# A hybrid decoder step: a planner that also keeps VectorE's time, and S5 steps cut into smaller units

## What is computed

```python
hn = rmsnorm(x, ln1_g)
proj = hn @ w_in                                    # q | k | v | u, 512 columns each
a = p[:, :, 0] - lam * p[:, :, 1]                   # differential attention, 4 heads, causal
...
_, h = lax.associative_scan(combine, (a, bu), axis=1)   # S5, 32 groups, 64 complex states
...
x = x + jnp.concatenate([attn, s5_out], axis=-1) @ w_out
x = x + hier_moe(rmsnorm(x, ln2_g), ...)            # 1 of 4 groups, 2 of 8 experts in it
```

## Time and profile before

| | us |
|---|---|
| median of 3 runs | 1464.19 (1458.98 to 1472.08) |
| the profiled execution | 1464.86 |
| its span, first to last instruction | 1463.1 |
| TensorE / VectorE / ScalarE busy | 1279.2 / 521.6 / 248.5 |

### The profile page before, as it was taken

How to read it: one execution, slowest core, us unless ns; L and a number is a source line. 1 busy time by engine, 2 the same in 40 slices (tenths; PEclk the granted TensorE clock), 3 DMA queues, 4 the chain that set the end, 5 groups by cost and what they waited for, 6 DMA issues and landing times.

```text
span 1463.1 us, 26568 instructions
## 1 busy us (share of the span) xinstructions
PE 1279.2 (87%) x9000; PEld 670.6 (46%) x9000; DVE 521.6 (36%) x1413; ACT 248.5 (17%) x476; POOL 214.7 (15%) x329
## 2 busy tenths in 40 slices
PE   7999999999869799998869999976899999999930
PEld 4545555554324346666544444433444444444410
DVE  2723543253365455553512111153122111121126
ACT  2101111121212233332212000000011111111111
POOL 2003140313100200000010000001122222222211
PEclk9999999999989999998999999976999999999975
DMA  9989998869968999999996998998899999999764
GB/s 364 329 310 293 321 294 283 272 198 298 298 227 304 352 338 363 365 315 323 331 387 228 330 336 293 322 349 321 277 324 371 360 354 363 361 363 366 256 211 179
DMA packets 185201, 458.31 MB, mean 313 GB/s; under 512 B 23953, under 2 KB 24337, under 8 KB 176530
## 3 DMA queue, kind: packets, MB, share of 16 engines
q1 hardware_dynamic: 163602, 390.21, 75.4%
q0 software_dynamic: 21504, 66.78, 13.8%
HBM read 421.92 MB, written 33.80 MB: 311 GB/s over the span
## 4 chain that ended last, share of the span: by engine, by line
PE 70%; DMA 12%; DVE 7%; SPq 5%; issue 3%; DVEq 2%; ACT 1%; POOL 0%; ACTq 0%; POOLq 0%
PE WA L1800 52%; PE SC L1800 7%; PE OD L1800 7%; DMA ring<-in_cacheK 6%; SPq L500 4%; DMA qpad<-h_scratch,idc 3%; DMA ring<-in_cacheV 2%; PE WA L2166 2%; DVE arena L1769 1%; PE WA L1919 1%; DVE arena L1782 1%; DVE st L1141 1%; PE WA L2126 1%; DMA arena<-y_scratch 1%; DVEq L1771 1%
## 5 line engine op out<-in xcount | busy, mean ns | idle before, releaser
L1800 PE MATMUL WA<-arena 128*128 128x512 f32 (+10 forms) x1440 | 353.4, 432 | 17.6 <-issue 7.2
L1800 PE MATMUL WA<-arena,xm 128*128 128x512 f32 (+3 forms) x816 | 313.6, 581 | 8.4 <-DMA arena<-in_w_out 6.5
L1800 PEld LDWEIGHTS WA<-arena 128*128 128x128 f32 (+2 forms) x1440 | 191.6, 195 | 155.0 <-issue 135.5
L1800 PEld LDWEIGHTS WA<-arena,xm 128*128 128x128 f32 (+1 forms) x816 | 124.4, 174 | 162.8 <-issue 154.7
L1800 PE MATMUL WA<-xm,arena 128*128 128x512 f32 x192 | 87.3, 603 | 1.7 <-ACT arena L958 1.3
L1800 PE MATMUL OD<-ring,sall 128*32 128x512 f32 x512 | 71.0, 670 | 15.0 <-DMA ring<-in_cacheV 15.0
L563 POOL TENSOR_TENSOR st<-st,consts 128x1 f32<-128x1 f32 (+2 forms) x18 | 13.8, 765 | 466.2 <-DVEq L1175 280.0
L1800 PE MATMUL OD<-ring,qpad 128*32 128x128 f32 x2048 | 67.9, 285 | 15.7 <-DMA ring<-in_cacheK 15.7
L1800 PEld LDWEIGHTS OD<-ring,qpad 128*32 128x32 f32 x2048 | 56.6, 114 | 35.9 <-DMA ring<-in_cacheK 18.4
L1800 PE MATMUL SC<-ring,qpad 128*32 128x128 f32 x2048 | 64.9, 278 | 9.1 <-DMA ring<-in_cacheK 9.0
L1712 DVE TENSOR_TENSOR xm<-WA,colw 128x960 f32<-128x960 f32 x16 | 18.5, 1158 | 147.2 <-PE WA L2166 147.2
(11 more groups left out here) (364 smaller groups left out, 1244.1 us busy)
## 6 DMA issues: line engine op xcount, KB each, us to landing
ring<-in_cacheK SPq DMA_DIRECT2D x512, 256.0 KB, 4.7
ring<-in_cacheV SPq DMA_DIRECT2D x512, 256.0 KB, 4.7
arena<-in_w_gu SPq DMA_DIRECT2D x16, 2048.0 KB, 9.8
arena<-in_w_dn SPq DMA_DIRECT2D x16, 1024.0 KB, 14.3
ring<-in_w_gu SPq DMA_DIRECT2D x8, 2048.0 KB, 10.3
xm<-in_w_gu SPq DMA_DIRECT2D x8, 2048.0 KB, 10.5
ring<-in_w_dn SPq DMA_DIRECT2D x8, 1024.0 KB, 14.8
xm<-in_w_dn SPq DMA_DIRECT2D x8, 1024.0 KB, 14.8
```

The lines of the kernel that those rows point to most:

```text
L1800: return pe.matmul(out, lhsT, rhs, start=first, stop=last, **kw)
```

## The change

- The planner now keeps a second clock, `busy`, for VectorE. `vector_us` gives each unit's time on VectorE and a lag from TensorE's end to its start; the end is written down as `("dve",) + unit`, and other units can name it as what they wait for. So a unit on VectorE is late when those ahead of it on VectorE are late.
- The lags in `streams` are cut down to what lies between VectorE's end and the next step. Some TensorE costs change (`O` from 0.37 to 0.21 per block, `bY` 3.5 to 4.1, `ids` 5.5 to 6.9).
- `hold` counts from VectorE's end where the unit has one.
- `s5a` becomes four units, `bA` two and `bH` three (`p` is the part). The instructions and their semaphores stay the same; between two parts other units may stand.
- ScalarE's order puts `S` by VectorE's end.

```diff
+def vector_us(unit):
+
+    k, a = unit[0], unit[1:]
+    i = a[0] if a else 0
+    if k in ("u", "k", "q", "out") and (len(a) == 1 or a[-1] == 1):
+        return {"u": (1.1, 0.2), "k": (1.25, 0.95), "q": (1.25, 0.95), "out": (0.75, 0.2)}[k]
+    return {
...
+        "S": (1.95 + 0.265 * i, 0.2), "C": (0.95 + 0.133 * i, 0.0), "O": (1.35 if a[1:] == (H - 1,) else 1.15, 0.2),
...
+        "bH": ((3.7, 3.0, 5.6)[a[1] if k == "bH" else 0], 0.0), "bY": (0.75, 0.9), "bG": (0.75, 0.8),
...
-        C.append((("C", i, h), 0.0, [(("S", i, h), 3.3 + 3.0 * w)]))
...
-        O.append((("O", i, h), 0.2 + 0.37 * (i + 1), x))
...
+        C.append((("C", i, h), 0.0, [(dve("S", i, h), 0.9 + w)]))
...
+        O.append((("O", i, h), 0.2 + 0.21 * (i + 1), x))
...
-    return {"S": 3.0 + 3.0 * w, "T": 0.5 + 0.8 * w, "O": 0.5, "pt": 1.3, "bY": 5.0, "bP": 1.5, "bK": 1.6,
-            "bX": 0.8, "q": 0.8, "k": 0.8, "v": 0.8, "hT": 1.5, "out": 1.0}.get(k, 1.0)
+    k, w = unit[0], 0.115 * (unit[1] + 1) if len(unit) > 1 else 0
+    return {"S": 0.7 + w, "T": 0.5 + w, "O": -0.5, "pt": 1.3, "bP": 1.5, "bK": 1.0, "out": 0.1, "u": 0.1, "hT": 0.1, "r": 0.1,
+            "bX": 0.8, "q": -0.4, "k": -0.4, "v": 0.9, "ot": 1.4, "glu": -0.8, "ids": 4.0, "rank": 16.0}.get(k, 1.0)
...
         t = max(t, ready) + cost
-        end[unit] = t
+        end[unit] = done = t
+        if vector_us(unit):
+            us, lag = vector_us(unit)
+            end[("dve",) + unit] = done = busy = max(busy, t + lag) + us
...
-                free[b] = t + hold(unit)
+                free[b] = done + hold(unit)
...
-    ready = {u: ends.get(u, ends.get(u[:-1], 0.0)) + (2.4 if u[0] == "S" else 0.0) for u in PLAN}
+    ready = {u: ends[("dve",) + u] - (0.9 + 0.13 * u[1]) if u[0] == "S" else ends.get(u, ends.get(u[:-1], 0.0)) for u in PLAN}
...
-            def bH(n):
+            def bH(n, p):
...
+                if p == 1:
+                    for j in range(JQ):
+                        decay = r8[:, JQ * n + j:JQ * n + j + 1].to_broadcast([128, NC])
+                        dve.tensor_tensor_scan(A[:, j, :], decay, X[1][:, j, :], 0.0, MUL, ADD)
+                        dve.tensor_tensor_scan(B[:, j, :], decay, X[0][:, j, :], 0.0, MUL, ADD)
+                    dve.drain()
+                    return
```

More of the change, by code:

```diff
@@ L125, in streams @@
         qs += [(("q", i, 0), half, x), (("q", i, 1), half, [])]
-    qt = [(("qt", i), 0.6, [(("q", i, 1), 3.5)] + ([(("S", i - 1, H - 1), 0)] if i else [])) for i in range(NT)]
+    qt = [(("qt", i), 0.5, [(dve("q", i, 1), 0.3)] + ([(("S", i - 1, H - 1), 0)] if i else [])) for i in range(NT)]
     S, C, T, O = [], [], [], []
@@ L144, in streams @@
+    s5 = [(("s5a", 0), 0.0, [(dve("dprep"), 0.0)])] + [(("s5a", p), 0.0, [(dve("s5a", p - 1), 1.3)]) for p in range(1, 4)]
     for n in range(NQ):
[L145 to L148, removed]
@@ L187, in make_plan @@
     land, gone, due = [4.0, 10.0], [], 4.0
-    kept, never = {}, 1e9
+    kept, never, busy = {}, 1e9, 0.0
     def place(unit):
@@ L226, in make_plan @@
         for b in kept.get(unit, []):
-            free[b] = t + 1.0
+            free[b] = done + hold(unit)
         if unit[0] in "KV":
@@ L1264, in cmul, with s5a_parts @@
                 dve.drain()
-            def s5a():
+            def s5a_parts():
                 dve.wait_ge(s_ld5, 32)
@@ L1329, in s5a @@
                 dve.drain()
+                yield
                 a, b = (v[7], v[6]), (v[18], v[19])
@@ L1354, in s5a, with bA @@
                     a, b = b, a
[L1356 to L1362 removed]
+                    if tab is T1 and k == 4:
+                        yield
+                yield
+            s5a_part = s5a_parts()
+            def s5a(p):
+                next(s5a_part)
+            def bA(n, p):
                 j = slice(JQ * n, JQ * n + JQ)
                 full = [128, JQ, CH, W5]
[L1365 removed]
                 Lj = [Lp[:, m, :, j].rearrange("p k j -> p j k") for m in range(2)]
[L1367 to L1369 removed]
+                if p == 0:
+                    if n:
+                        dve.wait_ge(*filled("Y", n - 1, 1))
+                    else:
+                        dve.wait_ge(*filled("u", 3, 1))
+                        dve.wait_ge(s_ust[1], 32)
+                    t = [tmp5[:, 512 * m:512 * m + 512].rearrange("p (j r h) -> p j r h", j=JQ, r=CH) for m in range(2)]
+                    cmul([PB[:, m, :, :, :] for m in range(2)],
+                         [bc[:, 0, m, j, :].unsqueeze(2).to_broadcast(full) for m in range(2)],
+                         [x[:, :, 0:CH].unsqueeze(3).to_broadcast(full) for x in Lj], t)
+                    dve.drain().then_inc(s_pA, 1)
+                    return
                 for m in range(2):
```

124 lines of the change are left out of this document (64 added, 60 removed), and 3 rows, old and new, of the table i.

## The result

The changed kernel takes 1476.46 us (median of 9 runs, 1473.44 to 1479.97) against 1464.19 for before (median of 9 runs, 1458.98 to 1472.08). The ratio is 1.0098, 95% interval 1.0071 to 1.0125. Run again beside other kernels (experiment e12) it is 1.0068 (1.0035 to 1.0101). So the change makes the kernel slower, by 0.7 to 1 %. The forecast was 1443 us, with 1467 as its upper end.

A forecast was written before the change was run, and what follows sets the result against it. The prediction took TensorE, busy 87% of the span, and its stalls as the bound. Terms -14.3 - 2.1 - 4 - 0 - 1.5 = -21.9 from 1464.9 gave 1443.0 us; own range 1433 to 1453, with rivals 1425 to 1467.

The forecast's parts named there:

- The third stage: Second K pass with the big heads: transfers set its length, TensorE's gain waits for pages; 0, bounds 0 and -7.
- What bounds the kernel now: Planned part: TensorE, busy 87%, idle 104.5 us; largest single stall 11.1 us, a long S5 unit ahead of attention.
- The T stalls: Transposes of weighted probabilities: all three waits go because bH(3) and bE(3) move ahead of the heads; -14.3 us.
- The clock: Matmuls just behind the 11.1 us stall: their slow running goes with the stall; -2.1 us, bounds 0 and 4.
- Page units earlier: K units of both passes: work moved behind them fills gaps where pages are late; -4 us, bounds 0 and -10.5.
- The last stage: Second V pass: an output half moves ahead, a V unit behind r(7); -1.5 us, bounds -5.5 and +3.
- A: Rival: pages take it back, K units wait longer by the 10.5 us they moved forward; 1457.5 us, chance 0.20.
- B: Rival: VectorE's waits get into the S5 chain, six units at 8.1 us; slower, 1491.6 us, chance 0.10.
- C: Rival: stage three's transpose waits (7 us) and 10 us of page waits go as well; 1426 us, chance 0.12.
- D: Rival: nothing moves, the stall goes and the next page unit waits as much; 1464 us, chance 0.08.
- The closing test of the prediction: Planned part: T waits gone and first second-pass K unit early, but same end, means stages three and four were misjudged.

The follow-up runs named there:

- e12: The changed kernel, unchanged, run once more beside the others on the same chip; 1474.66 us, ratio 1.0068.
- e11: The order of before with the last round's three bH parts spread behind C(1,0), C(1,1) and AN(0); 1458.72 us, ratio 0.9962.
- e15: e11 with bH(3)'s second part directly behind its first, both behind C(1,0); 1459.91 us, ratio 0.9975.
- e6: The changed kernel with `ids` one V unit later, so two V units stand behind it; 1470.84 us, ratio 1.0053.
- e14: The changed kernel with the edits of e13 and e6 together; 1459.59 us, ratio 0.9983.
- e13: The changed kernel with two V units of the first V pass (and ov(1)) one projection half later; 1470.57 us, ratio 1.0060.
- e10: The changed planner with VectorE's clock, but the parts of s5a, bA and bH placed directly behind one another; 1492.03 us, ratio 1.0170.
- e3: The order of before up to the first V unit of the second pass, the changed order behind it; 1473.47 us, ratio 1.0069.

## Why the prediction was wrong, point by point

The forecast was 21.9 us faster, the medians say 12.3 slower. By stages, in the profiled executions: up to the first K unit of the second pass -20.4 forecast and -12.0 found; to the first V unit of that pass 0 and +14.2; to the expert loop -1.5 and +5.7; the expert loop itself 0 and +0.7. Sum found +8.6. The third stage is taken here to the first V unit; 13 of its 14.2 us lie inside the K pass.

- *What bounds the kernel now.* The reading of the waits was right, and the largest single stall was what I said. The reading was incomplete in that it took TensorE's idle time as the thing to win. Idle time did fall, by 4.6 us over the span; busy time rose by 13.2.
- *The T stalls, -14.3.* The named wait went, as forecast, and no T waits between 380 and 440 us; the term failed in "the whole 14.3 us should go". T waits are 13.9 us in seven pieces. I had checked that nothing of S5 but one product of bG stands between S and C, but not how close the planner sets T behind C: its lag is now 0.25 us behind its own estimate of C's end. That these short lags make the seven waits is argued from the code, no run took them alone. And by e11 and e15 the stall with its clock is worth 3 to 7 us, less than half of the 16.4; a bank wait of 4.6 us that follows it in e11 may be part of the reason, which no run shows.
- *The clock, -2.1.* Wrong in sign. One slow stretch went with the stall (e11's clock in that stage is 0.97), and 2.1 us was a fair price for it, since it lay mostly on idle time. But short waits brought others in which TensorE works: 70 us at half clock before, 82 after.
- *Page units earlier, -4.* This is the step that failed most. I wrote that the work "isn't saved, it stands later, where pages are late and it can fill the gaps". Between the first K and the first V unit of the second pass TensorE stood 31.1 us before and 29.7 after; it filled 1.4 us and worked 15.6 longer, which is the 10.5 + 3.6 us moved there and little more. The first K unit came at 546.7, not at the 538 named, and the last router product 7.1 us earlier (957.0 against 964.1), not 21.
- *The third stage, 0.* The reason "what TensorE gains there it will wait for the next page" would hold only if the transfers were the limit. They weren't: with 15.6 us more busy time TensorE stood as long as before (30 us), so the stage grew by nearly all of it, 10.5 us of heads and the 3.6 of an output half. The issuing queue waited 27.2 + 15.0 us for it (16.4 + 8.3 before), and the rate fell from 332 to 310 GB/s for the same pages. That output half was missing in the sum: it was taken off the last stage and put on none.

```profile
SPq L528 <- PE SC L1851: 27.2, 13, 5.3
SPq L528 <- PE OD L1851: 15.0, 8, 6.0
```

- *The last stage, -1.5.* The bound of +3 was too small: +5.7 was found, or 9.3 with the 3.6 us of the output half that left the stage. The mechanism in it was the right one, V units behind the router product with two in the ring, but the place was the wrong one: not r(7), `ids`. Three V units behind it instead of two cost 4 to 6 us in e6 and 11 in e14 against e13, and the rows of before could have shown it: behind `ids` stand exactly the two units that the ring holds.
- *Rivals.* A: only in part; the first V unit was indeed not earlier, but K page waits rose only from 24.7 to 28.3 us (32.1 in e12) and the rate of the first stage rose. B: no wait at bY or bX names the scan; all that S5's parts hold up is one bK for 2.1 us. C: the third stage became longer, not shorter. D: its time is nearest to what came, but the stall was not swapped for a wait of the next page; the K unit came 12 us earlier. None of them was the slower case that came: many short waits with the low clock behind each, and one V unit too many behind a routing step. The closing test of the prediction did catch it: the stall gone, the first K unit early, the planned part not earlier, "then the step on stages three and four was wrong".

## What to carry to other kernels

A lead at one mark is only a gain if the same work has been done by then: compare busy time at each mark before calling earlier page units earlier. In an order that runs close to its transfers, page waits of one to four microseconds cost here about their length again in slow matmuls behind them (e13: 5.8 us less idle time, 6.9 less busy time), so idle time alone understates them. Whether the seven short waits of T cost more than the one long one that they replaced was not tested. And where a producer's ring holds n units, count how many consumers stand behind each long step that frees nothing: here n is 2, the third showed up as two waits of 3.4 and 2.2 us, and with six (e10) every one behind the second waited.

## What the runs showed that was not expected

- The spread of one kernel follows TensorE's clock. Three runs of e11: 1445.82 us at a granted clock of 0.949, 1454.86 at 0.942, 1466.43 at 0.940 (over all ten the correlation is -0.88). The same order had its first K unit of the second pass at 558.7 and at 564.8 us in two profiles (before and e3). A single profile can't judge a change of 5 us.
- Waits as short as 2.23 and 1.39 us, with work between them, were followed by a clock of 0.61 over 13 us (437 to 450 in after), and 1.23 and 3.61 at the other place by 0.59 over 12. At the first of these places e12 waited 1.18 and 2.29 us and had 0.74 over the next 13 us (449 to 462).
- At a DMA share of 1.04 the rate was 282 GB/s with S5's small transfers among the pages and 398 with larger ones from the same queue: the share alone doesn't say that pages come at full speed.
